# TensorE takes the attention steps two at a time in a hybrid decoder block

## What is computed

```
q, kc, vc, ksl, vsl, kwn, vwn, gate_logits, zu, zv = split(rms_norm(x) @ w_in)
o_attn = gates[0] * o_cmp + gates[1] * o_sel + gates[2] * o_win   # 8 heads, 2 groups of keys
o_mix  = gelu(zu) * (tril(sp_w) @ rms_norm(gelu(zv)) + sp_b)
x = x + concat(rms_norm(o_attn), rms_norm(o_mix)) @ w_out
x = x + square(relu(rms_norm(x) @ w_ff1)) @ w_ff2
```

## Time and profile before

| | us |
|---|---|
| median of 3 runs | 585.96 (584.51 to 586.27) |
| the profiled execution | 584.51 |
| its span, first to last instruction | 582.8 |
| PE busy | 567.6 (97%) |
| DVE busy | 440.9 (76%) |
| ACT busy | 357.8 (61%) |
| POOL busy | 129.4 (22%) |

### The profile page before, as it was taken

The page is one execution under the profiler, slowest core; times in us unless marked ns, Lnnn a source line. Parts: engine busy times, 40 slices in busy tenths (PEclk is TensorE's granted clock), DMA queues, the critical chain, the costliest instruction groups (busy, mean ns, idle before and its releaser), DMA issues.

```text
span 582.8 us, 9215 instructions
## 1 busy us (share of the span) xinstructions
PE 567.6 (97%) x3433; PEld 495.7 (85%) x3433; DVE 440.9 (76%) x721; ACT 357.8 (61%) x644; POOL 129.4 (22%) x209
## 2 busy tenths in 40 slices
PE   8999999999899999999999999999999999999997
PEld 6777777788677887879999999999988888888886
DVE  3799890686678899857868675566699996999674
ACT  6866661737667778845663486733696546646651
POOL 0560000002444454501220102312023033020200
PEclk9999999999999999999999999999999999999999
DMA  8933346341202111003997968997799889976862
GB/s 302 341 110 103 114 145 221 140 184 71 72 3 79 65 38 38 0 2 84 191 194 193 206 183 160 184 202 166 194 145 189 208 164 204 246 146 224 189 200 109
DMA packets 25164, 87.56 MB, mean 150 GB/s; under 512 B 3024, under 2 KB 3312, under 8 KB 25120
## 3 DMA queue, kind: packets, MB, share of 16 engines
q0 software_dynamic: 9856, 35.38, 33.1%
q1 hardware_dynamic: 15120, 51.59, 26.0%
q10 hardware_dynamic: 144, 0.00, 0.0%
HBM read 84.87 MB, written 2.10 MB: 149 GB/s over the span
## 4 chain that ended last, share of the span: by engine, by line
PE 82%; DVE 7%; DMA 3%; issue 2%; ACT 2%; POOL 2%; SPq 1%; DVEq 0%; ACTq 0%
PE ps L427 24%; PE ps L429 23%; PE ps L428 23%; PE ps L2071 2%; PE ps L2052 2%; DMA xT<-in_xt 2%; PE ps L1922 1%; DMA pe_sb<-in_cmp_pe 1%; DVE pt_sb L1524 1%; DVE w_lo_sb L1199 1%; PE ps L1779 1%; PE ps L2013 1%; PE ps L2014 1%; POOL rope_k L606 1%; DVE ps L1501 1%
## 5 line engine op out<-in xcount | busy, mean ns | idle before, releaser
L1039 ACT ACTIVATE w_hi_sb<-raw 128x1024 fp32r<-128x1024 f32 x112 | 118.6, 1060 | 115.2 <-PE ps L429 86.8
L1563 DVE TENSOR_TENSOR w_lo_sb<-raw,w_hi_sb 128x1024 fp32r<-128x1024 f32 x112 | 137.0, 1224 | 64.5 <-ACT w_hi_sb L1039 64.1
L680 POOL DMA_DIRECT2D raw<-in_w_ff x64 | 55.4, 866 | 237.6 <-DVE w_lo_sb L1563 213.4
L427 PE MATMUL ps<-w_hi_sb,a_hi 128*128 128x512 f32 x224 | 87.1, 389 | 0.0
L428 PE MATMUL ps<-w_lo_sb,a_hi 128*128 128x512 f32 x224 | 87.1, 389 | 0.0
L429 PE MATMUL ps<-w_hi_sb,a_lo 128*128 128x512 f32 x224 | 87.1, 389 | 0.0
L427 PE MATMUL ps<-w_hi_sb,ht_hi 128*128 128x512 f32 x192 | 78.7, 410 | 4.6 <-DVE xs L1555 1.6
L427 PE MATMUL ps<-ht_hi,w_hi_sb 128*128 128x256 f32 (+1 forms) x272 | 79.1, 291 | 0.0
L429 PE MATMUL ps<-ht_hi,w_lo_sb 128*128 128x256 f32 (+1 forms) x272 | 78.8, 290 | 0.0
L428 PE MATMUL ps<-ht_lo,w_hi_sb 128*128 128x256 f32 (+1 forms) x272 | 78.7, 289 | 0.0
L429 PE MATMUL ps<-w_hi_sb,ht_lo 128*128 128x512 f32 x192 | 75.2, 392 | 0.0
(11 more groups left out here) (238 smaller groups left out, 1139.5 us busy)
## 6 DMA issues: line engine op xcount, KB each, us to landing
raw<-in_w_ff POOLq DMA_DIRECT2D x64, 512.0 KB, 6.3
raw<-in_w_ff SPq DMA_DIRECT2D x48, 512.0 KB, 4.1
raw<-in_w SPq DMA_DIRECT2D x23, 512.0 KB, 4.4
xs<-in_x SPq DMA_DIRECT2D x8, 512.0 KB, 7.4
raw<-in_cmp_w SPq DMA_DIRECT2D x8, 512.0 KB, 4.4
xT<-in_xt SPq DMA_DIRECT2D x3, 512.0 KB, 9.1
raw<-in_w_c SPq DMA_DIRECT2D x4, 304.0 KB, 2.9
out_y<-xs SPq DMA_DIRECT2D x2, 512.0 KB, 2.9
```

The lines of the kernel that those rows point to most:

```text
L427: pe.matmul(out, l_hi, r_hi, start=start, stop=False)
L680: pool.dma_start(raw[:, n % RAW, :], (w_ff1, w_ff2)[stage - 1][k, q], accum_op=ALU.add, max_dma_last_dim=8192).then_inc(raw_added[n % RAW] ...
L1039: act.activation(w_hi_sb[:, FS[j], :], raw[:, j, :], ACT.Copy).then_inc(w_hi, 1)
L1563: dve.tensor_tensor(w_lo_sb[:, FS[j], :], raw[:, j, :], w_hi_sb[:, FS[j], :].bitcast(F32), ALU.subtract).then_inc(w_lo, 1)
```

## The change

PE's loop over the steps takes two of them per turn. In a turn with steps v and v + 1 it issues both scores, then both chunks (but the first chunk of a job and row transposes, `kept_back`), then both steps' transposes, then row transposes and turning back, then the values, then a first chunk. The same instructions are issued, and the lists of DVE, ACT, POOL and SP are as before.

```
-            for v in range(NV + LAG):
-                if v + LEAD < NV:
-                    scores(v + LEAD)
-                if v == 0:
+            def kept_back(v):
+
+                return v in CHUNKS and (CHUNKS[v][0] not in ADD_NO or CHUNKS[v][1] == 0)
+
+            for first in range(0, NV + LAG, 2):
+                pair = (first, first + 1)
+                for v in pair:
+                    if v + LEAD < NV:
+                        scores(v + LEAD)
+                if first == 0:
                     warm(WARM[1], JB)
-
-                product = CHUNKS[v] if v in CHUNKS and CHUNKS[v][0] in ADD_NO else None
-                if product and product[1] > 0:
-                    job(*product)
-                if v < NV:
-                    probs_t(v)
-                if v >= LAG:
-                    values(v - LAG)
-                if v in CHUNKS and (not product or product[1] == 0):
-                    job(*CHUNKS[v])
-                if v >= LAG + BACK and (v - LAG - BACK) % 4 == 3:
-                    turn_back((v - LAG - BACK) // 4)
+                for v in pair:
+                    if v in CHUNKS and not kept_back(v):
+                        job(*CHUNKS[v])
+                for v in pair:
+                    if v < NV:
+                        probs_t(v)
+                for v in pair:
+                    if kept_back(v) and CHUNKS[v][0] not in ADD_NO:
+                        job(*CHUNKS[v])
+                    if v >= LAG + BACK and (v - LAG - BACK) % 4 == 3:
+                        turn_back((v - LAG - BACK) // 4)
+                for v in pair:
+                    if v >= LAG:
+                        values(v - LAG)
+                for v in pair:
+                    if kept_back(v) and CHUNKS[v][0] in ADD_NO:
+                        job(*CHUNKS[v])
```

## The result

| | median, us | runs | ratio to before, 95% interval |
|---|---|---|---|
| before | 586.0 (584.51 to 586.27) | 4 | |
| after | 589.88 (589.57 to 591.2) | 4 | 1.0089 [1.0073, 1.0105] |

What follows compares the result with a forecast made beforehand. PE was taken as the bound from 183.7 us on, DVE close behind, with waits before that. Terms 3.25 + 1.0 + 0.75 + 1.1 = 6.1 us gave 590.6 or 592.1; forecast 591.3 us, 8-in-10 range 587.5 to 594.8.

Steps and rivals of the forecast that it cites:

- the forecast case: Whole kernel: late even-step transposes lengthen PE's waits, making it slower, 589 to 594 us; chance 0.61.
- the late head of the chain: Even-step transposes start later (0.92 us at step 20), delaying high part, low part, split and next low part PE awaits.
- Steps 4 and 8: Transposes 0.70 us late; next job's first chunk waits longer for `xs`, turning back fills some: 0.5 each, 1.0 us.
- Steps 12 to 19: No slot split; scores newly wait for the exponential at steps 19 and 23: 0.75 us for both, bounds 0 and 1.0.
- Steps 20 to 32: Slot splits at 20, 24, 28, 32 pass the lateness to PE: 0.92, 0.45, 1.03, 0.85, together 3.25 us.
- Steps 36 to 63: Lateness mostly absorbed, bursts on DVE and ACT: 1.1 us (0.6 around steps 42 and 47, 0.5 at 60).
- The side that could gain: Rival: turning back and row transposes fill PE's waits, 1.6 us won, up to 3; 583 to 584.3 us; chance 0.04.
- The clock: Rival: clock falls in a longer PE wait, work behind at half speed, +2 to +4 us, above 594; chance 0.01.
- The first: Sign: PE's transposes wait longer for the low part up to step 28, 2.3 us before, 4 or more after.
- The second: Sign: first chunks at steps 7 and 11 wait for `xs` about 0.7 us longer before turning back is taken off.
- The third: Sign: score products (L2013) appear as waiting for `p_sb`, 0.3 to 0.5 us at a time.
- the fourth: Sign: engines' busy times and matmul means stay; stretch from first feed-forward unit to the end stays 310 to 312 us.

Runs made afterwards that it cites:

- 1: Kernel before, with the transposes of all even steps moved right ahead of the odd step's, tail unchanged: 591.14 us, ratio 1.0103.
- 4: Kernel before, with only the tail of a turn changed (row transposes and turning back ahead of the values, first chunk behind): 584.15 us, ratio 0.9984.
- 11: Kernel after, with DVE's six slot splits cut to 64 of 512 columns (output weights' low parts incomplete): 585.61 us, ratio 1.0013 to before.
- 6: Kernel before, with DVE's six slot splits one step later, behind the odd step's low part: 586.29 us, ratio 1.0020.
- 7: Kernel after, with DVE's six slot splits one step later: 591.01 us, ratio 1.0107 to before.
- 10: Kernel before, with DVE's six slot splits cut to 64 of 512 columns (output weights' low parts incomplete): 581.71 us, ratio 0.9951.
- 13: Kernel before, with the changed tail and both even and odd steps' transposes ahead of their own chunks: 586.58 us, ratio 1.0030.
- 12: Kernel before, with the changed tail and only the even steps' transposes ahead of their own chunk: 585.18 us, ratio 1.0009.
- 8: Kernel before, with even steps' transposes held back by the next scores only, not by the chunk, so nothing is grouped: 586.2 us, ratio 1.0024.
- 5: Kernel before, with the changed tail as in 4, but row transposes behind the values again: 584.4 us, ratio 0.9983.

## Why the prediction was right

The time fell inside the forecast case (589 to 594 us), and the late head of the chain is the cause, as forecast: 1 and 4 show it. The path from there to PE was only in part the forecast one, and that the terms agree so well is in part luck. Where each term stands, by how much later the transposes of the odd steps start in the profile after (1.22 us taken off; starts of the weight loads of L2052 in both traces):

| steps | shift at the end | cost | forecast |
|---|---|---|---|
| 4, 8 (to step 13) | 0.87 | 0.9 | 1.0 |
| 12 to 19 (to step 21) | 1.37 | 0.5 | 0.75 |
| 20, 24, 28, 32 (to step 37) | 4.38 | 3.0 | 3.25 |
| 36 to 63 | 5.56 | 1.2 | 1.1 |

The sum is 5.6 against 6.1 in the profiled pair, of which 0.15 comes back behind step 63; it is 5.2 by the ratio and 3.9 between the medians.

- **Steps 20 to 32.** Right in sum, off in its parts, so the sum is luck: 0.5, 0.4, 0.8 and 1.3 where 0.92, 0.45, 1.03 and 0.85 were forecast. At step 20 the head was late as worked out: counted from the transposes of step 19 in either trace, the low part of 20 starts 0.90 us later than before. But the low part of 21 is only 0.62 later, for the split took 1.41 us in place of 1.67: POOL no longer scales at the same moment. The prediction held the splits' times fixed; all six together took 9.2 us before and 8.4 after. A further 0.1 came back because the values' wait for `ot_sb` (0.18 in the earlier trace rows) is gone. At step 32 the cost is larger than forecast, for at step 35 the row transposes did not fill a wait: they had 0.53 us of their own.
- **Steps 4 and 8.** Size right by luck, for the place is wrong. The prediction had the first chunks at 7 and 11 wait longer for `xs`; in fact they waited less than in the earlier trace rows, and the transposes ahead of them had the new wait, which the text had not given them:

```profile
152.90 0.30 PE L2052 MATMUL ps<-ident,p_sb 128*128 128x128 f32 x1 [0.56 <-DVE pt_sb L1524]
153.79 0.50 PE L427 MATMUL ps<-w_hi_sb,ht_hi 128*128 128x512 f32 x1 [0.36 <-DVE xs L1555]
```

- **Steps 12 to 19.** The new wait of the scores for `p_sb` is there, but smaller: 0.26 us a time with the slower second product, at steps 15 and 19 (forecast: 19 and 23), which makes the 0.5. It recurs at every second turn up to step 35. After step 20 it stands ahead of a longer wait and adds nothing, as forecast; 11 shows that it comes out when that one is gone.
- **Steps 36 to 63.** 1.2 us as forecast, and about where it was forecast (0.6 from step 37 to 49, 0.4 from 59 to 63), but by other waits. The row transposes behind steps 41 and 47 wait for `xs` (0.19 and 0.35 us). At step 61 the transposes start 0.22 us late and wait not for the scaled probabilities (done at 250.52) but for the low part of step 59, which ends at 250.71; they start at 250.82. The three rows of row transposes, the first that of step 35:

```profile
202.41 0.66 PE L1779 MATMUL ps<-ident,o_sb 128*128 128x128 f32 x4 [0.53 <-DVE xs L1555]
...
212.68 0.66 PE L1779 MATMUL ps<-ident,o_sb 128*128 128x128 f32 x4 [0.19 <-DVE xs L1555]
...
223.58 0.66 PE L1779 MATMUL ps<-ident,o_sb 128*128 128x128 f32 x4 [0.35 <-DVE xs L1555]
```

The prediction named no such wait. It is the tail's doing (4 has it too): before, the values stood ahead of these transposes and covered it.

- **The side that could gain.** Turning back ahead of a wait is worth something: 0.9 us in 4, of the 1.6 that the rival added up (3 with a share of the other waits), and the wait for turned rows shrank from 0.9 us to 0.7 only.
- **The clock.** No wait of PE in the four executions after cost clock. The 0.185 us a transpose at the start is a mean of two rates: of the 24 transposes 16 start 0.21 us apart, up to 4.9 us, and the rest 0.11.
- **The signs.** The first, the longer waits for the low part, came as said. The second did not: the first chunks waited less for `xs`, not 0.7 us more. The third came with 0.2 to 0.3 us at a time. Of the fourth, the stretch behind the attention stayed, but PE's busy time rose from 567.6 to 570.6 us, the short waits that count as busy. The earlier trace rows were also read short: PE's waits in the attention were 6.3 us in the list, not 5.3, with 0.7 for `ot_sb` and 0.3 more for the low part.
- **The reason as written** was half of it. It put the loss on the split that is queued between the two low parts. 6 and 7 show that its place is indifferent, 10 and 11 that about a third of the loss needs its length (with a wide margin, and hardly any behind step 13). The rest comes through ACT, whose exponential stands behind the late high part, and through DVE's row maximum to ACT's copy of the turned values.

What stays open: how much of the loss at steps 4 and 8 needs the split, for the profiled execution of 11 has the drop of the clock there; and what, besides 0.3 us of waits, makes 13 slower than 12.

## What to carry to other kernels

When an engine hands work to others that run strictly in order and are nearly as full, moving its hand-over later can cost up to what it is late (0.53 of 0.92 us at step 20, nothing of 0.23 in 8), even if the engine itself arrives at the answer no earlier; moving it sooner gives nothing where the receiver's own list stands still. Look at the idle time in front of the receiving instruction: it rose from 0.69 us to 1.75 at step 20, where the wait of the bounding engine rose from 0.63 to 1.00 only. And look at the distances between products: half of the loss was in no listed wait. A reordering is best split into its parts and each timed: here the part that fills waits (0.9984) was hidden under one that costs 1.0%.

## What the hardware showed

**The granted clock drops for 3 to 4 us in about half of the executions of the kernel before.** Of the 24 executions of the kernel before in the last comparison, 13 had a mean clock of 0.999 or 1.000 and a median of 584.16 us, 11 one of 0.996 or 0.997 and 585.55 us: 1.4 us, more than the tail's gain. (That gain is there within each group: 4 has 583.49 against 584.21 us, and 584.93 against 585.82.) The profiles of 5, 6, 7, 11, 12 and 13 have the drop, each between 146 and 152 us. The profiles of 6 and of the kernel before show the place, around the first attention steps:

```profile
144.00:146.00 2.00, 0.42 (x2) 0.14 (x1) 1.78 (x5) 1.88 (x10) 0.00 (x0) 1.00 0.00 0
146.00:150.00 4.00, 3.91 (x13) 3.05 (x14) 1.28 (x7) 2.29 (x8) 2.17 (x6) 0.60 0.02 4
...
144.00:146.00 2.00, 0.87 (x6) 0.45 (x4) 1.46 (x5) 1.88 (x9) 0.26 (x1) 1.00 0.16 57
146.00:150.00 4.00, 3.46 (x21) 2.91 (x20) 2.44 (x9) 3.25 (x13) 2.50 (x6) 1.00 0.00 0
```

In 6 PE had been busy 0.42 of 2.00 us and the clock then went to 1.2 GHz; in the kernel before it had been busy 0.87 of 2.00 and kept 2.4. But 13 fell after 0.84 of 2.00 and 4 kept the clock after 0.36, so these rows don't say what tips it. All four executions of the kernel after kept the clock, while the median before lies with the longer kind, which flatters the kernel after by up to 1.4 us; 7 and 11, with its order of PE, have the drop in their profiles.

**DVE's split is slower while POOL scales probabilities.** Its two operations take 1.67 us at 172.11, when POOL's scaling (171.48, 1.10) is still running, and 1.41 after the change, when that had ended at 174.89. The Trainium skill, SBUF — State Buffer, Terms, has DVE and GpSimd take turns at a shared pair of ports, the loser blocked for a whole instruction; with 0.47 us of overlap and 0.26 us lost the trace agrees in kind. In 8 the overlap at the same step is 0.26 us and 0.05 us is lost; before, at 179.59, it is 0.21 us and nothing is lost (1.41).
